# Hybrid layer with 32 experts on one core: descriptor scratch of 4 KB, a ninth down-weight place loaded early, expert 1's rows turned behind expert 0's product

## The reference

```python
h = layer_norm(alpha * h + hybrid_token_mixer(h, ...), ln1_g, ln1_b)
# hierarchical_moe(h): top-1 group of 4, then top-2 of its 8 experts
hg = jnp.einsum("td,edf->tef", t, exp_w_gate)      # 32 x 1024 x 256
hu = jnp.einsum("td,edf->tef", t, exp_w_up)        # 32 x 1024 x 256
hid = jax.nn.silu(hg) * hu * combine[:, :, None]
out = jnp.einsum("tef,efd->td", hid, exp_w_down)   # 32 x 256 x 1024
h = layer_norm(alpha * h + out, ln2_g, ln2_b)
```

## Time and profile before

| | |
|---|---|
| median of 3 runs | 449.0 us (448.27 to 450.28) |
| the profiled execution | 447.62 us |
| its span, first to last instruction | 445.8 us |
| mean granted TensorE clock | 0.977 |
| TensorE busy | 412.4 us (93%) |
| VectorE, ScalarE, GpSimd busy | 187.4, 114.3, 83.5 us |
| moved by DMA | 139.10 MB, mean 312 GB/s |

### The profile page before, as it was taken

The page is one execution under the profiler, slowest core; times in us unless marked ns, Lnnn a source line. Parts: engine busy times, 40 slices in busy tenths (PEclk is TensorE's granted clock), DMA queues, the critical chain, the costliest instruction groups (busy, mean ns, idle before and its releaser), DMA issues.

```text
span 445.8 us, 6662 instructions
## 1 busy us (share of the span) xinstructions
PE 412.4 (93%) x2594; PEld 276.0 (62%) x2594; DVE 187.4 (42%) x375; ACT 114.3 (26%) x185; POOL 83.5 (19%) x112
## 2 busy tenths in 40 slices
PE   7999999999999999889999999999987979787891
PEld 6788877888888888755555555655544435443330
DVE  2659522799954485745222221222211111211085
ACT  4443388942150014101111111111101101111411
POOL 2500000000000001013333223332222123200133
PEclk9999999999999999999999999999989889998996
DMA  8866522022399999789999999999999999998583
GB/s 266 258 176 195 184 94 96 0 94 96 97 346 389 412 420 392 305 297 413 411 407 401 369 410 410 407 410 411 411 410 413 412 414 412 412 415 354 192 326 141
DMA packets 45568, 139.10 MB, mean 312 GB/s; under 512 B 5351, under 2 KB 17671, under 8 KB 41446
## 3 DMA queue, kind: packets, MB, share of 16 engines
q1 hardware_dynamic: 39376, 126.89, 73.5%
q0 software_dynamic: 6144, 11.84, 7.2%
q10 hardware_dynamic: 22, 0.02, 0.0%
HBM read 134.41 MB, written 12.58 MB: 330 GB/s over the span
## 4 chain that ended last, share of the span: by engine, by line
PE 70%; DMA 18%; DVE 6%; SPq 3%; issue 1%; ACT 0%; DVEq 0%; ACTq 0%; POOLq 0%
PE bank L1083 18%; PE bank L904 11%; PE bank L906 11%; PE bank L905 11%; DMA wdn<-in_exp_w_down 10%; PE bank L1102 9%; DMA wgu<-in_exp_w_up 5%; PE bank L1071 2%; PE bank L1093 2%; DMA raw<-in_w_in 2%; PE bank L1157 2%; SPq L503 2%; DMA xg<-h_rows,x_rows 1%; DVE stats L1522 1%; PE bank L1011 1%
## 5 line engine op out<-in xcount | busy, mean ns | idle before, releaser
L1083 PE MATMUL bank<-wgu,xTg 128*64 128x256 f32 x960 | 111.9, 386 | 7.1 <-DMA wgu<-in_exp_w_up 6.7
L1083 PEld LDWEIGHTS bank<-wgu,xTg 128*64 128x64 f32 x960 | 67.2, 139 | 42.7 <-DMA wgu<-in_exp_w_up 7.2
L1102 PE MATMUL bank<-wdn,hidT 128*64 128x512 f32 x248 | 61.3, 616 | 8.1 <-DMA wdn<-in_exp_w_down 7.7
L904 PE MATMUL bank<-xT_hi,w_hi 128*128 128x512 f32 x160 | 63.0, 394 | 1.7 <-DVE xT_lo L1206 1.7
L906 PE MATMUL bank<-xT_hi,w_lo 128*128 128x512 f32 x160 | 62.3, 389 | 0.0
L905 PE MATMUL bank<-xT_lo,w_hi 128*128 128x512 f32 x160 | 62.3, 389 | 0.0
L679 POOL DMA_INDIRECT y_pairs<-ys,y_rows x32 | 32.6, 1018 | 146.2 <-PE bank L1071 95.1
L1478 DVE TENSOR_TENSOR hid<-gated,bank 64x256 f32<-64x256 f32 x32 | 13.5, 423 | 104.9 <-ACT gated L839 104.9
L839 ACT ACTIVATE gated<-bank 64x256 f32<-64x256 f32 x32 | 12.1, 379 | 142.2 <-PE bank L1083 142.2
L1183 DVE TENSOR_TENSOR w_lo<-raw,w_hi 128x2048 fp32r<-128x2048 f32 x12 | 27.5, 2288 | 26.9 <-ACT w_hi L753 26.9
L1102 PEld LDWEIGHTS bank<-wdn,hidT 128*64 128x64 f32 x248 | 17.2, 137 | 32.0 <-issue 18.4
(11 more groups left out here) (242 smaller groups left out, 437.2 us busy)
## 6 DMA issues: line engine op xcount, KB each, us to landing
wdn<-in_exp_w_down SPq DMA_DIRECT2D x31, 1024.0 KB, 20.4
wgu<-in_exp_w_gate SPq DMA_DIRECT2D x30, 1024.0 KB, 14.9
wgu<-in_exp_w_up SPq DMA_DIRECT2D x30, 1024.0 KB, 18.4
raw<-in_w_in SPq DMA_DIRECT2D x9, 1024.0 KB, 5.3
raw<-in_w_out SPq DMA_DIRECT2D x4, 1024.0 KB, 5.0
pair_y<-y_pairs SPq DMA_DIRECT2D x8, 512.0 KB, 7.6
xres<-in_x SPq DMA_DIRECT2D x4, 512.0 KB, 7.5
h_rows<-xres POOLq DMA_DIRECT2D x4, 512.0 KB, 7.8
```

The costliest lines, as they stand in the source:

```text
L904: pe.matmul(dst, a_hi, b_hi, start=start, stop=False)
L1083: mm = pe.matmul(psum[2 + b][BLOCK * which:BLOCK * which + BLOCK, 0:F], xTg[b][:, j, h * BLOCK:(h + 1) * BLOCK], wgu[s][:, which, k, :], s ...
L1102: mm = pe.matmul(psum[6 + b][BLOCK * n:BLOCK * n + BLOCK, :], hidT[b][:, j, :], wdn[s][:, j, n * H:(n + 1) * H], start=j == 0, stop=j == 1)
```

## The change

It does five things. The scratch that holds GpSimd's DMA descriptors shrinks from 16 KB per partition to 4 KB. In the 12 KB that this frees, `wdn_extra` gets 8 KB: a down-weight place for expert 7, which is loaded directly behind expert 0's weights. With as many first places for down as for gate/up, one slot function serves both, and SP's order has gate/up only one expert ahead of down. Expert 1's rows are turned behind expert 0's gate product instead of in its middle. In the router, the last tile's first half is turned before the tile before it is multiplied, and each router product waits for the halves one by one. On GpSimd, three waits stand between the small loads at the start.

```diff
-DN_FIRST = RING + 1
-GU_FIRST = RING + 2
+FIRST = RING + 2
...
+        wdn.append(at("wdn_extra", [P, 2, D], F32, spare + 16384))
...
-        def gu_slot(q):
-            return q if q < GU_FIRST else (q - 2) % RING
-
-        def dn_slot(q):
-            return q if q < DN_FIRST else (q - 1) % RING
+        def slot_of(q):
+            return q if q < FIRST else (q - 2) % RING
...
             load_gu(0, 0, gu_in[0])
             load_dn(0, 0, dn_in[0])
+            load_dn(RING + 1, RING + 1, dn_in[RING + 1])
...
+            def used_by(q, r):
+
+                return q + r * RING - (FIRST if static(r) and q < FIRST + RING else RING)
...
-            LEAD = 2
-            head = GU_FIRST + RING - LEAD + 1
-            turns = (N_EXP - LEAD - head) // RING
-            refill_gu(GU_FIRST, 0)
-            for q in range(DN_FIRST, head):
-                refill_gu(q + LEAD, 0)
+            head = FIRST + RING
+            turns = (N_EXP - 1 - head) // RING
+            refill_gu(FIRST, 0)
+            for q in range(FIRST, head):
+                refill_gu(q + 1, 0)
                 refill_dn(q, 0)
...
             pool.dma_start(ln_b[:, :], row(ln1_b).to_broadcast([P, D])).then_inc(ln1_in, 16)
+            pool.wait_ge(gates_in, 32)
+            pool.wait_ge(ln1_in, 32)
             pool.dma_start(wr[:, :, 0:N_GROUPS], router_group_w.rearrange("(k p) n -> p k n", p=P)).then_inc(router_in, 16)
+            pool.wait_ge(router_in, 16)
             pool.dma_start(wr[:, :, N_GROUPS:NR], router_expert_w.rearrange("(k p) n -> p k n", p=P)).then_inc(router_in, 16)
...
-                pe.wait_ge(h1T_ready, 2 * t + 2)
                 for k in range(KT):
+                    if k % 4 == 0:
+                        pe.wait_ge(h1T_ready, 2 * t + k // 4 + 1)
...
             router(TT - 3)
+            turn_h1(TT - 1, (0,))
             router(TT - 2)
-            turn_h1(TT - 1)
+            turn_h1(TT - 1, (1,))
             router(TT - 1)
...
-                gate_up(q + r * RING, gu_slot(q), q % 2, 2, gu_loads(q, r),
-                        amid=(lambda: turn_main_x(1, 0)) if q == 0 else None)
+                gate_up(q + r * RING, slot_of(q), q % 2, 2, loads_of(q, r))
                 if q == 0:
+
+                    turn_main_x(1, 0)
                     return
...
-    nc = _bacc.Bacc("TRN2", target_bir_lowering=False, num_devices=1)
+    nc = _bacc.Bacc("TRN2", target_bir_lowering=False, num_devices=1, dynamic_dma_scratch_size=4096)
```

More of the change, by code:

```diff
@@ L182, in hybrid_moe_layer @@
         wdn.append(wdn_first)
-        assert spare + 16384 <= nc.sbuf_usable_end, (spare, nc.sbuf_usable_end)
+        wdn.append(at("wdn_extra", [P, 2, D], F32, spare + 16384))
+        assert spare + 24576 <= nc.sbuf_usable_end, (spare, nc.sbuf_usable_end)
         raw = [at(f"raw{b}", [P, CHUNK], F32, spare + 8192 * b) for b in range(2)]
@@ L291, in hybrid_moe_layer @@
         router_in = sem("router_in")
-        gu_in = [sem(f"gu_in{s}") for s in range(GU_FIRST)]
-        dn_in = [sem(f"dn_in{s}") for s in range(DN_FIRST)]
+        gu_in = [sem(f"gu_in{s}") for s in range(FIRST)]
+        dn_in = [sem(f"dn_in{s}") for s in range(FIRST)]
         over_gu_in = sem("over_gu_in")
@@ L420, in gu_place, with loads_of @@
             return wgu[s][:, which, :, :].rearrange("p (h j) f -> p h (j f)", h=2)
-        def gu_slot(q):
-            return q if q < GU_FIRST else (q - 2) % RING
-        def dn_slot(q):
-            return q if q < DN_FIRST else (q - 1) % RING
[L433 to L439, removed]
+        def slot_of(q):
+            return q if q < FIRST else (q - 2) % RING
+        def loads_of(q, r):
+            return r + (1 if q < FIRST else (q - 2) // RING + 1)
         def rounds(engine, body):
-            head, turns = GU_FIRST, (N_EXP - 1 - GU_FIRST) // RING
+            head, turns = FIRST + 1, (N_EXP - 1 - (FIRST + 1)) // RING
             for q in range(head):
@@ L559, in _ @@
                 for u in range(RING):
-                    refill_gu(head + u + LEAD, r)
+                    refill_gu(head + u + 1, r)
                     refill_dn(head + u, r)
[L564 to L567, removed]
+            for q in range(head + turns * RING, N_EXP):
+                if q + 1 < N_EXP:
+                    refill_gu(q + 1, 0)
                 refill_dn(q, 0)
-                if q + LEAD < N_EXP:
-                    refill_gu(q + LEAD, 0)
-            last_of_1 = max(q for q in range(N_EXP) if gu_slot(q) == 1)
+            last_of_1 = max(q for q in range(N_EXP) if slot_of(q) == 1)
             sp_.wait_ge(gu_summed, last_of_1 + 1)
@@ L991, in _, with turn_h1 @@
                 pe.wait_ge(w_lo_ready, c + 1)
-            def turn_h1(t):
+            def turn_h1(t, halves=(0, 1)):
                 if t >= 2:
                     pe.wait_ge(h1T_ready, 2 * (t - 1))
-                for n in range(2):
+                for n in halves:
                     pe.wait_ge(h1_ready, 2 * t + n + 1)
@@ L1072, in turn_x, with gate_up @@
                 mm.then_inc(xg_turned, 1)
-            def gate_up(i, s, b, lag, loads, amid=None):
+            def gate_up(i, s, b, lag, loads):
                 pe.wait_ge(gu_in[s], 32 * loads)
@@ L1078, in gate_up @@
                 for k in range(KT):
-                    if amid and k == KT // 2:
-                        amid()
                     h, j = divmod(k, 4)
@@ L1109, in main_down @@
             def main_down(q, r):
-                down(q + r * RING, dn_slot(q), q % 2, 2, dn_loads(q, r))
+                down(q + r * RING, slot_of(q), q % 2, 2, loads_of(q, r))
             def pe_item(q, r):
@@ L1140, in pe_over @@
                 i = j + N_EXP
-                loads = [j + 1 + sum(of(q) == 0 for q in range(N_EXP)) for of in (gu_slot, dn_slot)]
+                loads = j + 1 + sum(slot_of(q) == 0 for q in range(N_EXP))
                 turn_x(i, 0, 0, 1, x_gathered[0], 16 * j + mains(0))
-                gate_up(i, 0, 0, 1, loads[0])
+                gate_up(i, 0, 0, 1, loads)
                 turn_hid(i, 0, 1)
-                down(i, 0, 0, 1, loads[1])
+                down(i, 0, 0, 1, loads)
             overflow(pe, pe_over)
```

10 lines of the change are left out of this document (4 added, 6 removed).

## The result

The changed kernel takes 442.83 us (median of 4 runs, 442.45 to 443.09) against 448.87 (448.27 to 450.28) beside it: ratio 0.986, 95% interval 0.9836 to 0.9885. The profiled execution took 442.45 us, its span 440.7, and 1.8 lie around it as before. The new place is the eighth for a down weight (seven before; the title counts it as the ninth).

The account below looks back on a forecast made before the run. The weight stream was taken to set the end: its last hold plus the bytes left. From the profiled 447.62, less 2.55, 0.84 and 0.30, came 443.9, or 445.3 on the timed runs' scale; range 443.0 to 448.0.

Parts of the forecast that it names:

- Waits and a smaller ring on GpSimd: GpSimd's small loads at the start and its descriptor scratch: waits lie in idle time, issues stay 1.02 us, cost 0.
- The tail moves as a whole: End of the kernel: the work behind the last up weight shifts with its landing, 3.7 us less on the timed scale.
- Only the last hold counts: Weight stream: losses before SP's stop ahead of gate/up 14 only shift when it runs dry, so they do not matter.
- the 2.55: Weight stream behind SP's stop: expert 7's early down weight leaves one weight less to carry, 2.55 us saved.
- The order of the refills: SP's queue: gate/up one expert ahead of down meets the same waits and makes no new dry place, cost 0.
- Expert 1's turn, 0.84 through TensorE: TensorE near 190 to 200 us: turning rows behind expert 0's product ends expert 1's product 0.84 us earlier.
- rival 2: Gather of expert 1 or 3 lands late and eats TensorE's 1.1 us; only the megabyte counts: 446.4 us, chance 0.13.
- makes the stream only dry earlier at the stop: Gate/up of expert 8, issued some 2.6 us earlier, closes most of the second hole but brings nothing at the stop.
- The router, 0.30: Last token tile's router product: 16 of 32 products run before the second copy, 0.3 us saved, bounds 0 and 0.5.
- Rival 4: Last gate product: a shorter wait ahead restores TensorE's clock, another 1.5 us back, 443.8 us, chance 0.07.
- SP's issue of gate/up 14: Sign for the forecast in SP's queue: this issue comes some 1.1 us earlier, near 244.4 us.
- TensorE's wait for rows: Sign against the forecast: TensorE waiting for gathered rows between 194 and 245 us.

Follow-up runs that it names:

- The early drain on 16 KB: Kernel before, 16 KB ring kept, one more drain of GpSimd's queue added in front of its wait for the second LayerNorm's loads: 445.96 us, ratio 0.9938.
- the waits alone: Kernel before with its 16 KB ring and only the three new waits among GpSimd's small loads: 448.16 us, ratio 0.9979.
- The order alone: Kernel before with only SP's refill order changed, gate/up one expert ahead of down, no extra place: 449.59 us, ratio 1.0029.
- those two runs: Kernel before with gate/up one expert ahead of down, without and with an added early drain of GpSimd's queue: 449.59 and 447.85 us.
- the late load: Kernel after with expert 7's down weight loaded behind gate/up 8 and 9, extra place kept, run twice: 443.76 and 444.63 us.
- the old order on after: Kernel after with SP's refill order as before, gate/up two ahead; with the old end too: 445.57 us, with the new end: 446.43 us.
- three buffers: Kernel after with three buffers for gathered rows in place of two, run twice: 442.65 and 442.11 us.
- the kernel after in group 2: Kernel after unchanged, run again as the measure for undoing the turn or the router halves: 443.58 us, ratio 0.988.

## Why the prediction was off

**Where the gain comes from.** The small ring 2.5 us (448.38 to 445.90); place, early load and order 2.1 (445.90 to 443.84); the turn 0.9 (444.50 to 443.58), the router none. The sum is 5.5; the medians of the kernel after are 4.9 to 6.1 under those of before beside them. The prediction had 2.55, 0.84 and 0.30, and nothing for the ring. These shares come from pairs of runs, and only the 2.5 and the 2.1 are clear of their intervals.

**The step that failed first: "Waits and a smaller ring on GpSimd ... I take nothing", with "The tail moves as a whole".** Issues stayed at 1.02 us and the waits cost nothing (last small load issued at 32.2), as written. But the ring also sets how long GpSimd's last drain takes, and that drain ended the span. The early drain on 16 KB shows it; the waits alone show nothing of it. The chain of waits was read up to the last gate product and not to the last instruction; this step alone puts the time under the range. Without its 2.5 us the time would be 445.3, the forecast itself; but that the other terms add up so well (3.0 measured, 3.7 forecast) is in part luck, as the next paragraphs tell.

**"Only the last hold counts" was wrong**, and with it the reason for the 2.55. The order alone carries down 12 ahead of the stop, the hold that I let decide, and is slower. What counts is all the time in which the stream is not full, wherever it lies. Lost against 411 GB/s over 134 to 150, 170 to 180, 186 to 208 and 238 to 254 us: before 0.5 + 0.7 + 5.9 + 1.4 = 8.5; order alone 0.5 + 0.9 + 6.5 + 0.1 = 8.0, and 0.4 more between 208 and 238; after -0.2 - 0.1 + 3.3 + 2.5 = 5.5 (below zero is above 411). Before less after is 3.0, and the landing came 2.6 sooner from the mark. The other traces bear this out. Summed over seven windows from 9 to 275 us behind the mark, they lose between 4.6 and 9.7 us; and in the 19 traces whose last expert waits for its up weight, the landing (in us behind the mark) less this sum is the same within 1.2 us, 271.7 to 272.9. For the order alone the sum says no gain, though its dip at the stop is gone; the runs say 1.5 us slower, and the cause of that stays open: in both traces with this order that difference is at the upper end (272.8 and 272.9), in the kernel before at the lower (271.7).

**"The order of the refills ... Cost 0" was wrong both ways.** The three stream edits belong together. One gate/up ahead puts down 12 in front of the stop, but without the extra place it holds gate/up 9 behind expert 0's down product; those two runs were 1.5 and 1.9 us slower than their partners. With the place gate/up 9 is not held (199.45). The extra place and the early load without the order are 2 to 3 us above the kernel after, though no run of it stood beside them. The early load gives about 1 us of the whole, by filling places ahead of 186 us that the prediction took for full (381 GB/s at 170 to 180, 397 at 134 to 150 before; 414 and 416 below). With the late load these places are open again, by 1.2 and 0.5 us in the second run.

```profile
134.00:150.00 16.00, 16.00 (x73) 13.23 (x72) 6.97 (x9) 0.00 (x0) 0.00 (x0) 1.00 1.02 416
170.00:180.00 10.00, 9.71 (x173) 8.70 (x172) 6.81 (x32) 4.74 (x8) 1.09 (x3) 1.00 1.01 414
```

**Expert 1's turn, 0.84 through TensorE:** the mechanism failed, the size held by accident. Its product starts at 195.75 (forecast 195.74), but this execution runs 0.23 us ahead of before at the mark. Counted from there, TensorE is done with expert 1's product 0.5 us earlier than before (74.3 against 74.9); in the two other executions of the kernel after it is 0.6 and 0.0, the last with expert 1's own rows waited for (0.60 us). The turn and the copy took 1.70 us, not 1.59. Then rival 2 came, at the place it named: expert 3's gather took 7.76 us, over the bound of 7.0 from the earlier trace rows, and its rows were waited for. Expert 8's gate product started 116.7 us behind the mark before and 117.1, 116.5 and 116.9 in the three executions of the kernel after; only the old order on after (116.0, 116.1) and three buffers (116.0) were clearly earlier. The 0.9 us came through the earlier gate/up 8, of which the prediction said that it "makes the stream only dry earlier at the stop"; some of it is kept. On the kernel before, where the same two edits stood alone, no gain can be told from nothing.

**The router, 0.30:** wrong, it brings nothing. The last product seems to end 0.24 us earlier (177.24, before 177.48), but the whole execution is 0.23 earlier at the mark. From the mark the product ends at 52.2 in all traces, with and without halves, and expert 0's gate product starts at 65.3. The step that was mis-sized is the second half's copy: it ends 51.5 us behind the mark instead of 51.0, 0.5 later where the prediction had some 0.2, and that takes all that the earlier first 16 products save.

```profile
175.82 1.42 PE L1005 MATMUL bank<-wr,h1T 128*64 128x36 f32 x32
175.93 0.60 ACT L816 ACTIVATE h1T<-bank 128x512 f32<-128x512 f32 x1 [1.05 <-PE bank L993]
```

**Rival 4, the clock.** In the profiled executions the last gate product took 5.11 us before and 3.67 after. This is what the rival described, with 0.62 us of wait ahead of it instead of 2.27. But the kernel after in group 2 took the slow one:

```profile
403.81 5.36 PE L1076 MATMUL bank<-wgu,xTg 128*64 128x256 f32 x32 [2.28 <-DMA wgu<-in_exp_w_up]
```

In the 20 traces the product took 3.67 us behind waits of at most 0.62 us (9 traces), and behind waits of 2.2 to 2.3 us 5.1 to 5.4 (9 traces; before, at a clock of 0.68 from 405 to 410 us) or 3.67 (2 traces). Both waits are found in executions of the kernel after, so this is not shown to be part of the change. From the mark, the last down product ends 1.7 us later in that execution, the last store is issued 0.9 later: ahead of the sums with h1 TensorE waits 2.35 us in the quick execution, for h1, and 1.66 in this one, for ScalarE.

**What was to show it.** Right: 348 GB/s over 188 to 200 us (237 in the first 4 of them), the deeper dip at the stop (2.4 us lost), no second dip. Not as forecast: SP's issue of gate/up 14 (244.4 expected, 245.75 measured), the landing (401.5, 402.36), and TensorE's wait for rows, which was named as a sign against. The Trainium skill ("DMA: Bandwidth & Descriptors", section Where 436 GB/s comes from) gives about 358 GB/s as what the HBM side allows a core; it isn't the limit in this kernel, which runs on one core: 411 from 250 to 400 us again.

## What to carry to other kernels

Read the chain to the very last instruction, the drains behind the last store included, before an edit to a queue is priced at nothing. Where the end waits for a stream of loads, each microsecond in which the stream isn't full counts, wherever it lies; so add up its open places over the whole run instead of taking the last hold. And look at a fixed order of issues together with the waits in it: what moves one load ahead of a stop can hold back the load behind it. And compare two traces from a mark in both: 0.23 us of offset looked like the router's gain.

## What the hardware showed that I had not expected

GpSimd's last drain took less with a smaller ring of descriptors, and less when the queue had been drained before: 7.52 us with 16 KB (in four kernels the same within 2 ns), 2.46 with 4 KB, 2.22 with 8 KB, 2.78 with 4 KB and three buffers for rows, and with 16 KB and an early drain 6.38 there and 1.37 at the end. It looks as if the drain goes over what has not been cleared since the start; that is inferred from the sum (7.75 us) staying about the same, and no run looked inside. Why 8 KB takes no longer than 4 KB stays open too.
